# Scores on the whole array with zero-padded keys, and grouped values as one product of 256 columns

## What is computed

```
def gqa_block(q, k, v):                     # 8 query heads, 2 key heads, head size 64
    s = jnp.einsum('bqkgd,bskd->bkgqs', q, k).astype(jnp.float32) * (HEAD_DIM ** -0.5)
    p = jax.nn.softmax(s, axis=-1).astype(v.dtype)
    return jnp.einsum('bkgqs,bskd->bqkgd', p, v)

def diff_block(q, k, v, lam):               # 4 heads, two maps each, values of 128
    s = jnp.einsum('bqhmd,bshmd->bhmqs', q, k).astype(jnp.float32) * (HEAD_DIM ** -0.5)
    p = jax.nn.softmax(s, axis=-1)
    p = p[:, :, 0] - lam * p[:, :, 1]
    return jnp.einsum('bhqs,bshe->bqhe', p.astype(v.dtype), v)
```

## Time and profile before

| | us |
|---|---|
| median of 3 runs | 2390.17 |
| lowest, highest | 2383.72, 2390.27 |
| profiled execution | 2387.86 |
| its span, first to last instruction | 2386.1 |
| PE busy in the span | 2310.7 (97%) |
| DVE busy | 1495.4 (63%) |
| ACT busy | 1065.7 (45%) |

### The profile page before, as it was taken

One profiled execution on the slowest core, in us unless ns is written; L12 is line 12 of the kernel. 1 busy time (PEld: TensorE's weight loads), 2 busy tenths in 40 slices (PEclk: granted clock), 3 DMA queues, 4 the chain that ended last, 5 costly groups with the idle time before them and its releaser, 6 DMA issues. The chain is left out here.

```text
span 2386.1 us, 40526 instructions
## 1 busy us (share of the span) xinstructions
PE 2310.7 (97%) x16311; PEld 2139.7 (90%) x16311; DVE 1495.4 (63%) x2403; ACT 1065.7 (45%) x2121; POOL 194.7 (8%) x160
## 2 busy tenths in 40 slices
PE   7999999899999999999999999999999999999999
PEld 5877877799999999999997777778999999999998
DVE  5335568677664865747643565787676658467473
ACT  5433357644442642524346333674444345344252
POOL 1330000100003000000215200010000110000000
PEclk9999999999999999999999999999999999999999
DMA  9225440122225223232231163102222432323222
GB/s 299 96 68 172 143 152 28 45 80 80 75 94 159 63 79 88 81 98 68 93 125 53 51 199 120 33 1 71 80 80 80 159 81 73 105 62 98 65 73 84
DMA packets 246666, 224.01 MB, mean 94 GB/s; under 512 B 6945, under 2 KB 232305, under 8 KB 245969
## 3 DMA queue, kind: packets, MB, share of 16 engines
q1 hardware_dynamic: 242528, 219.25, 29.7%
q0 software_dynamic: 480, 0.66, 0.3%
q10 hardware_dynamic: 3472, 1.52, 0.2%
HBM read 211.70 MB, written 9.70 MB: 93 GB/s over the span
## 5 line engine op out<-in xcount | busy, mean ns | idle before, releaser
L2352 ACT ACTIVATE ring_high<-raw 128x512 fp32r<-128x512 f32 (+1 forms) x278 | 158.1, 609 | 250.0 <-PE ps L2706 150.4
L2492 DVE TENSOR_TENSOR ring_low<-raw,ring_high 128x512 fp32r<-128x512 f32 (+1 forms) x278 | 204.5, 761 | 69.3 <-ACT ring_high L2352 65.1
L2771 PE MATMUL ps<-hH,ring_low 128*128 128x320 f32 x640 | 197.9, 309 | 0.3
L2771 PE MATMUL ps<-hH,ring_high 128*128 128x320 f32 x640 | 197.8, 309 | 0.0
L2771 PE MATMUL ps<-hL,ring_high 128*128 128x320 f32 x640 | 197.8, 309 | 0.0
L1564 DVE SCALAR_TENSOR_TENSOR xT<-ps,mod,xT 128x512 f32<-128x512 f32 (+1 forms) x128 | 64.0, 545 | 193.4 <-PE ps L2706 193.4
L359 PE MATMUL ps<-wH,hL 128*128 128x512 f32 (+1 forms) x460 | 176.5, 384 | 5.2 <-DVE wL L871 2.6
L359 PE MATMUL ps<-wH,hH 128*128 128x512 f32 (+1 forms) x460 | 171.0, 372 | 0.0
L2706 PE MATMUL ps<-gH,ring_low 128*128 128x320 f32 x704 | 160.9, 310 | 0.3 <-DVE xT L1564 0.3
L2706 PE MATMUL ps<-gL,ring_high 128*128 128x320 f32 x704 | 160.4, 309 | 0.0
L2706 PE MATMUL ps<-gH,ring_high 128*128 128x320 f32 x704 | 160.3, 309 | 0.0
(11 more groups left out here) (384 smaller groups left out, 6194.8 us busy)
## 6 DMA issues: line engine op xcount, KB each, us to landing
raw<-in_w_in SPq DMA_DIRECT2D x56, 1024.0 KB, 5.4
raw<-in_w_ffn_in SPq DMA_DIRECT2D x88, 512.0 KB, 5.2
gmod<-in_w_mod SPq DMA_DIRECT2D x24, 1024.0 KB, 8.6
raw<-in_w_ffn_out SPq DMA_DIRECT2D x16, 1024.0 KB, 5.1
b_raw<-in_w_branch SPq DMA_DIRECT2D x22, 512.0 KB, 4.4
head_w<-in_w_mod SPq DMA_DIRECT2D x8, 1024.0 KB, 12.4
modw<-in_w_mod SPq DMA_DIRECT2D x8, 1024.0 KB, 7.6
raw<-in_w_out SPq DMA_DIRECT2D x8, 1024.0 KB, 5.8
```

What stands on the lines that cost most here:

```text
L2352: nc.scalar.activation(ring_block(m.ring_high, b, src.shape[1], src.shape[2]), src, ACT.Copy).then_inc(m.sem("w_high"), 1)
L2492: nc.vector.tensor_tensor(ring_block(m.ring_low, b, nk, cols), src, ring_block(m.ring_high, b, nk, cols).bitcast(F32), ALU.subtract).then_ ...
L2771: last = nc.tensor.matmul(m.ps[:, plan.banks[n, 0][BANK[what]], 0:HALF], w[:, k, :], a[:, k, :], start=(first and k == 0 and q == 0), stop ...
```

## The change

- Each key block gets two buffers of 128 rows: `k_low` with the low half's key and zeros below, `k_high` with the high half's key and zeros above. A score product now takes all 128 rows of the query block against one of them; the zeros cancel the other half. Per step there are still four products, of 384, 256, 256 and 384 columns, all on the whole array, one after the other in PSUM columns 128 to 1407 of the set. The wait on `tail_scored` is gone.
- GQA values: five products instead of ten. The weights are all 128 columns of the values (both key heads), and 256 columns move, the weight maps of both query heads. Half of the result is not used. ACT copies the wanted 64 rows out with two instructions where one was.
- The diff weighing is one instruction of 640 columns instead of 512 and 128.
- In `project_attention`, ACT copies the lower 64 rows of each transposed key block, DVE the upper 64 (6 new copies a layer), and POOL zeroes twelve blocks of 64 x 768. ACT's wait for the stores of the differential keys is gone. Space comes from a smaller scratch area for POOL's DMAs; `gmod` moves and is loaded in two halves.
- The small parameters are loaded by SP, right behind weight slab 1 of `head`.

```diff
+        spare = [at(f"k{i}", [P, TT + 1, P], 3072 * i) for i in range(6)]
+        self.k_low = {"gqa": [self.kv[:, 8, :, :], self.kv[:, 10, :, :]], "diff": [x[:, :, :] for x in spare[2:6]]}
+        self.k_high = {"gqa": [spare[1][:, :, :], spare[0][:, :, :]],
+                       "diff": [at(f"k_high{j}", [P, TT + 1, P], front + 3072 * j)[:, :, :] for j in range(4)]}
...
+        @block.gpsimd
+        def _(pool):
+            zeroed = m.sem("keys_zeroed")
+            for x in m.k_high["gqa"]:
+                pool.memset(x[0:HD, :, :], 0.0).then_inc(zeroed, 1)
...
+                for turn in {6: (8, 9), 8: (10, 11, 12, 13)}.get(s, ()):
+                    kind, _, j = k_of[turn - first_k]
+                    dve.wait_ge(m.sem("turned"), turn + 1)
+                    src = m.ps[:, 6:8, :].rearrange("p b c -> p (b c)")[HD:P, 0:(TT + 1) * P]
+                    nc.vector.tensor_copy(m.k_high[kind][j][HD:P, :, :].rearrange("p t c -> p (t c)"), src
+                                          ).then_inc(m.sem("high_copied"), 1)
...
+                            if turn > first_k:
+                                pe.wait_ge(m.sem("high_copied"), turn - first_k)
...
-                    nc.tensor.matmul(m.ps[:, b + 1, 0:P], m.rq[low, qb, pos, :], m.kv[low, kb[0], TT, :],
-                                     start=True, stop=True).then_inc(m.sem("tail_scored"), 1)
-                    nc.tensor.matmul(m.ps[:, b + 2, :], m.rq[high, qb, pos, :],
-                                     m.kv[high, kb[1], 0:4, :].rearrange("p t c -> p (t c)"), start=True, stop=True)
-                    nc.tensor.matmul(m.ps[:, b, :], m.rq[low, qb, pos, :],
-                                     m.kv[low, kb[0], 0:4, :].rearrange("p t c -> p (t c)"), start=True, stop=True)
-                    pe.wait_ge(m.sem("tail_scored"), sum(x[1] < CTX for x in steps[:s + 1]))
-                    last = nc.tensor.matmul(m.ps[:, b + 1, 384:512], m.rq[high, qb, pos, :], m.kv[high, kb[1], TT, :],
-                                            start=True, stop=True)
+                    q = m.rq[:, j, POS[qt], :] if kind == "gqa" else m.rq[:, 4 + j, qt, :]
+                    k = j // 2 if kind == "gqa" else j
+                    for keys, first, n, to, at in ((m.k_low, 0, 3, b, P), (m.k_low, 3, 2, b + 1, 0),
+                                                   (m.k_high, 0, 2, b + 1, 2 * P), (m.k_high, 2, 3, b + 2, 0)):
+                        last = nc.tensor.matmul(m.ps[:, to, at:at + n * P], q,
+                                                keys[kind][k][:, first:first + n, :].rearrange("p t c -> p (t c)"),
+                                                start=True, stop=True)
...
-                    v = slice(j // 2 * HD, (j // 2 + 1) * HD)
                     for n in range(5):
-                        for half in range(2):
-                            last = nc.tensor.matmul(out[half * HD:(half + 1) * HD, 0:P], m.kv[:, 9, KEYS[half][n], v],
-                                                    eT[:, 5 * half + n, :], start=(n == 0), stop=(n == 4))
+                        last = nc.tensor.matmul(out[:, 0:2 * P].rearrange("p (h c) -> p h c", h=2), m.kv[:, 9, KEYS[n], :],
+                                                eT.rearrange("p (h t) c -> p h t c", h=2)[:, :, n, :],
+                                                start=(n == 0), stop=(n == 4))
...
-                        ins = nc.scalar.activation(m.rq[:, j, POS[qt], :], bank(c)[:, n * P:(n + 1) * P], ACT.Copy)
+                        rows = slice(j // 2 * HD, (j // 2 + 1) * HD)
+                        for half in range(2):
+                            ins = nc.scalar.activation(m.rq[half * HD:(half + 1) * HD, j, POS[qt], :],
+                                                       bank(c)[rows, (n + half) * P:(n + half + 1) * P], ACT.Copy)
...
+                if n == 1:
+                    small_params(sp)
```

More of the change, by code:

```diff
@@ L182, in __init__ @@
         self.g_e = [at(f"g_e{i}", [P, T], x1 + 2560 * i) for i in range(2)]
-        self.gmod = [at(f"gmod{j}", [P, KT, W256], 8192 * j) for j in range(2)]
-        self.gmrow = at("gmrow", [P, W256], 16384)
+        front = -15360
+        self.gmod = [[at(f"gmod{j}{r}", [P, 4, W256], x) for r, x in enumerate(pair)]
+                     for j, pair in enumerate(((front, front + 4096), (front + 8192, x0 + 57344)))]
+        self.gmrow = at("gmrow", [P, W256], front + 12288)
         self.g_s = [at(f"g_s{u}", [P, NCH, P], 5120 * u) for u in range(4)]
@@ L258, in sem @@
         if name not in self.sems:
[L259 to L262, removed]
+            pool, used = self.sem_sets[self.turn], len(self.sems)
             if len(pool) == used:
@@ L429, in mod_groups @@
             last = nc.tensor.matmul(m.ps[MG * g:MG * g + MG, bank, 0:W256], m.scw[:, 4 * r + g, first:first + MG],
-                                    w[:, 4 * r + g, :], start=(j == 0 and r == 0), stop=(r == 1), skip_group_check=True)
+                                    w[r][:, g, :], start=(j == 0 and r == 0), stop=(r == 1), skip_group_check=True)
     return last
@@ L944, in project_attention @@
              6: [(c, m.kv, 8 + 2 * c, TT + 1, 1, 5) for c in range(2)],
-             8: [(c, m.kv, c, TT + 1, 2 + c // 2, 6 + c // 2) for c in range(4)]}
+             8: [(c, m.kv, c, TT + 1, 0, 6 + c // 2) for c in range(4)]}
+    k_of = [("gqa", 0, 1), ("gqa", 1, 0)] + [("diff", j, j) for j in range(4)]
+    first_k = sum(len(turns[s]) for s in (3, 4, 5))
     def consumed(s):
@@ L990, in _ @@
                     sp.wait_ge(m.sem(f"attention_mod{j}"), 16)
+        @block.gpsimd
[3 more added lines that the diff above has]
+                pool.memset(x[0:HD, :, :], 0.0).then_inc(zeroed, 1)
+            for x in m.k_low["diff"]:
+                pool.memset(x[HD:P, :, :], 0.0).then_inc(zeroed, 1)
+            for j, x in enumerate(m.k_low["gqa"]):
+                pool.wait_ge(m.sem("turned"), first_k + j + 1)
+                pool.wait_ge(m.sem("k_stored0"), 16)
+                pool.memset(x[HD:P, :, :], 0.0).then_inc(zeroed, 1)
+            pool.wait_ge(m.sem("mod_used"), len(mods))
+            for x in m.k_high["diff"]:
+                pool.memset(x[0:HD, :, :], 0.0).then_inc(zeroed, 1)
+            pool.wait_ge(zeroed, 12)
         @block.scalar
@@ L1137, in mod @@
             def mod(j):
-                pe.wait_ge(m.sem(f"mod_loaded{j % 2}"), 16 * (j // 2 + 1))
-                mod_groups(nc, m, m.gmod[j % 2], 5, j).then_inc(m.sem("mod_used"), 1)
+                pe.wait_ge(m.sem(f"mod_loaded{j % 2}"), 32 * (j // 2 + 1))
+                mod_groups(nc, m, [half[:, :, :] for half in m.gmod[j % 2]], 5, j).then_inc(m.sem("mod_used"), 1)
             for s in range(begin, n):
@@ L1311, in scores @@
                             if kind == "ctx gqa":
-                                qb, pos, kb = j + i, POS[CTX], ((8, 10), (10, 8))[j // 2][half]
+                                qb, pos, k = j + i, POS[CTX], (m.k_low, m.k_high)[half]["gqa"][j // 2]
                             else:
-                                qb, pos, kb = 4 + j + i, CTX, j + i
+                                qb, pos, k = 4 + j + i, CTX, (m.k_low, m.k_high)[half]["diff"][j + i]
                             last = nc.tensor.matmul(m.ps[:, b + 2 * half, i * P:(i + 1) * P], m.rq[h, qb, pos, :],
-                                                    m.kv[h, kb, CTX, :], start=True, stop=True)
+                                                    k[h, KEY_AT[CTX], :], start=True, stop=True)
                 last.then_inc(m.sem("scores"), 1)
@@ L1516, in out @@
                 kind, qt, j = steps[s]
-                if kind == "gqa":
-                    return nc.vector.tensor_copy(m.rq[:, j, POS[qt], :], src[:, 0:P])
                 if kind == "diff":
```

71 lines of the change are left out of this document (36 added, 35 removed).

## The result

| | us |
|---|---|
| before, median of 4 | 2390.22 |
| changed, median of 4 (2458.29 to 2461.7) | 2459.39 |
| ratio | 1.0294, 95% interval 1.0272 to 1.0317 |
| predicted | 2457, range 2446 to 2472 |
| profiled execution of the changed kernel | 2458.29, span 2456.5 |

What follows compares the result with a forecast made beforehand. The prediction took PE, busy for 97% of the span, to bound the kernel. Scores +47.4, GQA values +25.0, idle time -6.7 and projection +1.4 sum to +67.1 us on 2390.2: 2457 us, range 2446 to 2472.

Steps and rivals of the forecast that it cites:

- The bound: Attention pairs: PE busy for 7.01 of 7.01 us, DVE 6.10, ACT 5.19; PE's instructions set the pair's time.
- The price of a column: PE's F32 records: 0.833 ns a column on the whole array as on halves, plus 0.005 us a record.
- the upper bound from the F32R rows: Cost per PE record beyond streaming: at most 0.013 us, from F32R records of 512 columns; lower bound 0.
- Scores: Attention scores: 2.17 us a step against 1.43, for 64 steps +47.4 us.
- GQA values: Attention's gqa values: ten records of 256 columns, 2.18 us against 1.40, for 32 steps +25.0 us.
- Rival 1: Attention products: the whole array streams F32 faster than its halves; -22 us, 2369, chance 0.04.
- The passages: Changes of array shape on PE in the pairs: 0.15 us a round trip, alone a gain of 14 us over 96.
- ACT's second copy: Behind gqa values: about 0.3 us a pair, hidden by PE at no cost; without that cover 10 us.
- The idle time: PE's idle time in both attention stages takes up 6.7 of 14.7 us, bounds 0 and -14.7.
- The projection: End of the projection stage: PE's transposes wait for DVE's first key copy, +1.4 us, bounds 0 and 2.5.
- The head: Fourteen small loads moved from POOL to SP between weight slabs 1 and 2: cost 0, bounds -1 and +3.
- The prediction's own sign of being wrong: Profile after: 384-column record about 0.33 us, pairs over 9.5 us with PE idle, or stages outside attention changing over 3 us.

Runs made afterwards that it cites:

- short_values: Kernel before with values over two of five key tiles in gqa and diff steps, result not the reference's; 2360.30 us, ratio 0.9872.
- values_ahead: Kernel before with the gqa values moved ahead of the one transpose in the last chunk of each diff step; 2387.17 us, ratio 0.9988.
- changed_one_copy: Changed kernel with one ACT copy of 128 rows behind the gqa values instead of two, omitting one query head's result; 2454.51 us, ratio 1.028.
- values_one_copy: Kernel before with only GQA values changed to five products, and one ACT copy, omitting one query head's result; 2413.58 us, ratio 1.0105.
- head_only: Kernel before with the fourteen small loads on SP behind weight slab 1 and nothing else; 2385.98 us, ratio 0.9987.
- changed_again: Changed kernel run once more, unaltered, for its clock records; 2456.61 us in a single execution.
- attention_back: Changed kernel with scores and values on half arrays as before, reading the new key buffers; 2389.71 us, ratio 1.0002.

## Why the prediction was right

**The bound.** It read PE as busy for all of a pair, with DVE next at 6.1 us. The pairs of the changed kernel and of short_values show both: PE's extra time comes out one for one (9.23 us for a predicted 9.27), and below about 6.2 us DVE holds.

**The price of a column.** The step that decided the sign was that the whole array streams F32 at the price its halves do, 0.833 ns a column, so that giving up the two halves at once doubles the streaming time. The trace of before had this only from products with one full direction. Measured: 0.323 us for 384 columns, 0.216 for 256, so about 0.003 us beyond the streaming, not the 0.005 that was taken; the upper bound from the F32R rows is not reached. Scores: 4 x 0.323 + 4 x 0.216 = 2.156 for a predicted 2.17, +46.5 us for +47.4. GQA values: 2.161 for 2.18, and from 1.245 + 0.15 before that is +24.5 for +25.0. Rival 1 is out. Doubled streaming did not double the sections: 2.16 against 1.28 + 0.15 is a factor of 1.5, as is 2.16 against 1.25 + 0.15. A section of 640 columns twice on each half would stream in 1.07 us at this price and took 1.28 and 1.25. What this 0.2 us is, no run here takes apart; the prediction had it inside its 1.28 and 1.25, so its sum did not need to know.

**The passages.** 0.15 us a round trip, saved 96 times, fits: in the pair they are gone from the timeline, and values_ahead saves one at a time. The rule of the Trainium skill, "TensorEngine Tiling (Array Packing)", section "Key Properties", that a change of mode drains the array agrees with the 0.15 us of a passage from and to the whole array; from row halves to column halves no cost shows here.

**ACT's second copy** was put down as hidden. In the pairs it is, but not beside modulation products and at the ends of the stages, where it cost about 3.5 us (changed_one_copy). On the kernel before, with shorter scores, it would have cost 10 (values_one_copy), which is what the prediction named as its price without cover.

**The idle time** was said to take up 6.7 us of 14.7. The attention grew by 70.1 us against 71.0 of array time, so 0.9 net; with 3.5 us of the second copy in the profiled stages taken out, the cover was about 4.4 us. PE's idle time says the same: 19.1 us in the two whole stages before, 18.9 now, 15.4 with one copy. At the start of layer 1 the wait came out shorter, as described, and the clock stayed up. Whether it stayed up because of the shorter wait is open. In all four profiles with long scores PE waits 1.12 us there and the clock stays up; in the eight with scores on row halves it waits 2.19 us, and the clock falls in five and stays up in three. With unchanged attention and no fall, this stage takes 132.4 us (head_only) instead of 133.6. So 1.2 of the 4.4 us would have come without the change in some executions.

**The projection** was put at +1.4 us. PE's waits for DVE's first copy are 0.8 and 1.1 us longer than before (a copy takes 0.96 us); from the changed kernel, the wait of layer 0, in the place of the earlier trace rows:

```profile
307.95 0.96 DVE L1160 COPY k_high<-ps 64x768 f32<-64x768 f32 x1
...
309.06 0.85 PE L1206 MATMUL ps<-cst,kv 128*128 128x128 f32 x6 [0.96 <-DVE k_high L1160]
```

That is +1.9 by the mechanism named. The profiled run has +5.3 over both layers; the clock, which the prediction didn't think of, is about 1.8 in layer 0. The rest in layer 1 is open: there the projection took 1.9 us longer than before in changed_again with a fall of the clock, and 1.8 longer in attention_back without one.

**The head** was put at 0 with bounds of -1 and +3, and this term missed them: -4.8 us in the profiled run. The prediction asked whether SP has room for fourteen issues and not who waits for these loads. DVE did, for 5.35 us, with the split of a weight slab queued behind. The prediction's own sign of being wrong, stages outside `attention` that change by more than 3 us, is met here: -4.8 us in the head, and +5.3 in the two projections together. The attention stages themselves, said to be about 34 us longer each, are 37.6 and 32.5 longer.

So the large terms were right by their mechanism, and that the total hit within 2.4 us is in part luck, because side terms cancel: the head 4.8 us below, the projection 3.9 above, cover and copy together 5.8 above, the array's time 1.4 below (67.1 - 4.8 + 3.9 + 5.8 - 1.4 = 70.6, the span's growth being 70.4). The array's time alone, 71.0 us, would have given 2461, also inside the range.

## What to carry to other kernels

When an engine is busy for all of a steady step, price a change by what it adds to that engine's starts, column by column, and check the next engine's busy time for how far a gain could go. Two half-array products that ran side by side streamed at twice the rate, and with all that a section costs, 0.15 us for getting in and out of the shape included, they were worth a factor of 1.5 here: zeros in the other half throw that away. And when a load is moved, look first for who waits for it and what is queued behind that wait.

## What was not expected of the hardware

A direct passage from products on row halves to products on column halves showed no cost, while each passage by way of the whole array had 0.15 us (values_ahead). After a wait of PE of some 2 us the clock sometimes fell to the 1.2 GHz level for 3.4 us and sometimes did not, in the same kernel at the same place (changed kernel and changed_again, behind 1.99 and 2.17 us).
